# Float32 products of a first projection split into three float32r products each, with low parts and a power table on GpSimd

## The reference

```python
h = rms_norm(x, even_mix_norm[j])
proj = jnp.einsum('bld,de->ble', h, even_in_proj[j])        # 1024 -> 512 + 4 x 512
u = proj[..., :S5_WIDTH]                                    # state-space mixer
hq, hf, hi, hg = jnp.split(proj[..., S5_WIDTH:], 4, axis=-1) # query, forget, value, gate
a_out = s5_mixer(u, s5_lambda_re[j], ...)     # diagonal complex scan, powers of A in tables
b_out = hgrn2_mixer(hq, hf, hi, hg, lower_bounds[layer], hgrn_o_norm[j])
mix = jnp.einsum('bld,de->ble', jnp.concatenate([a_out, b_out], axis=-1), even_out_proj[j])
...
x = x + mix   # then a mixture of 16 experts; then layer 1: windowed attention and 16 experts
```

## Time and profile before

| what | value |
|---|---|
| time, median of 3 runs (lowest to highest) | 841.51 us (840.99 to 843.66) |
| profiled execution, first to last instruction | 839.3 us |
| instructions | 11097 |
| busy: PE, DVE, ACT, POOL | 788.2, 599.7, 467.4, 165.9 us |
| mean granted TensorE clock | 0.982 |
| chain that ended last: PE, DMA, DVE, ACT, POOL | 51%, 22%, 14%, 8%, 1% |

### The profile page before, as it was taken

One profiled execution on the slowest core, in us unless ns is written; L12 is line 12 of the kernel. 1 busy time (PEld: TensorE's weight loads), 2 busy tenths in 40 slices (PEclk: granted clock), 3 DMA queues, 4 the chain that ended last, 5 costly groups with the idle time before them and its releaser, 6 DMA issues.

```text
span 839.3 us, 11097 instructions
## 1 busy us (share of the span) xinstructions
PE 788.2 (94%) x4236; PEld 553.6 (66%) x4236; DVE 599.7 (71%) x817; ACT 467.4 (56%) x637; POOL 165.9 (20%) x169
## 2 busy tenths in 40 slices
PE   5999999999999899988998999999999899999992
PEld 3455555555688878867876555556579778777771
DVE  4699974766553879877996466757635798797890
ACT  5033202814333488786885118676735488697781
POOL 4400001400001222322211001033102223234121
PEclk9999999999999899999999999999998899999997
DMA  9422020203453499989986300142064599999952
GB/s 370 155 91 73 30 101 1 101 1 138 192 211 125 164 421 357 333 316 313 329 306 229 125 0 1 37 165 100 1 276 166 207 397 351 316 320 333 325 162 33
DMA packets 31451, 160.94 MB, mean 192 GB/s; under 512 B 7601, under 2 KB 7729, under 8 KB 16032
## 3 DMA queue, kind: packets, MB, share of 16 engines
q1 hardware_dynamic: 18432, 130.03, 40.6%
q0 software_dynamic: 11232, 24.60, 10.4%
q10 hardware_dynamic: 1728, 5.52, 1.7%
HBM read 152.32 MB, written 24.12 MB: 210 GB/s over the span
## 4 chain that ended last, share of the span: by engine, by line
PE 51%; DMA 22%; DVE 14%; ACT 8%; POOL 1%; issue 1%; DVEq 0%; ACTq 0%; SPq 0%; POOLq 0%
DMA ring<-stream 21%; PE PS L1795 11%; DVE w_lo L992 9%; PE PS L1982 8%; PE PS L2231 7%; PE PS L1761 3%; ACT w_hi L686 3%; PE PS L2012 2%; PE PS L2137 2%; PE PS L2112 2%; PE PS L2266 2%; PE PS L1927 2%; PE PS L2289 1%; PE PS L2045 1%; PE PS L1745 1%
## 5 line engine op out<-in xcount | busy, mean ns | idle before, releaser
L992 DVE TENSOR_TENSOR w_lo<-ring,w_hi 128x2048 fp32r<-128x2048 f32 x92 | 210.0, 2290 | 40.8 <-ACT w_hi L686 37.4
L686 ACT ACTIVATE w_hi<-ring 128x2048 fp32r<-128x2048 f32 x86 | 164.7, 1917 | 47.2 <-DMA ring<-stream 43.4
L2112 PE MATMUL PS<-w_hi,left_hi 128*128 128x512 f32 x512 | 174.4, 402 | 6.1 <-DVE w_lo L992 3.7
L2112 PEld LDWEIGHTS PS<-w_hi,left_hi 128*128 128x128 f32 x512 | 96.2, 188 | 29.2 <-DVE w_lo L992 6.0
L2112 PE MATMUL PS<-w_lo,left_hi 128*128 128x512 f32 x256 | 100.2, 391 | 0.0
L2137 PE MATMUL PS<-w_hi,left_lo 128*128 128x512 f32 x256 | 85.3, 394 | 9.6 <-DVE left_lo L992 8.4
L2231 PE MATMUL PS<-ring,hT 128*128 128x512 f32 (+1 forms) x192 | 74.6, 534 | 0.0
L536 POOL DMA_INDIRECT arena<-rows x32 | 49.6, 1549 | 122.8 <-PE PS L2089 108.6
L2137 PEld LDWEIGHTS PS<-w_hi,left_lo 128*128 128x128 f32 x256 | 48.1, 188 | 22.4 <-DVE left_lo L992 11.0
L1795 PE MATMUL PS<-ring,hT 128*128 128x512 f32 x128 | 57.6, 599 | 0.4 <-ACT arena L732 0.4
L1795 PE MATMUL PS<-hT,ring 128*128 128x512 f32 x128 | 56.3, 595 | 0.0
(11 more groups left out here) (274 smaller groups left out, 1373.2 us busy)
## 6 DMA issues: line engine op xcount, KB each, us to landing
ring<-stream SPq DMA_DIRECT2D x110, 1024.0 KB, 16.3
arena<-stream SPq DMA_DIRECT2D x6, 1024.0 KB, 8.1
rows<-arena POOLq DMA_DIRECT2D x8, 512.0 KB, 3.0
x<-stream SPq DMA_DIRECT2D x4, 1024.0 KB, 6.6
x<-x_in SPq DMA_DIRECT2D x4, 512.0 KB, 5.5
x<-x_in ACTq DMA_DIRECT2D x4, 512.0 KB, 4.5
sums<-x POOLq DMA_DIRECT2D x4, 512.0 KB, 3.8
x<-sums SPq DMA_DIRECT2D x4, 512.0 KB, 5.2
```

What stands on the lines that cost most here:

```text
L686: act.activation(w_hi[pair], held_slot(layer, m), ACT.Copy).then_inc(w_hi_done, 1)
L992: return V.tensor_tensor(out, a, b, op)
L2112: ins = mm(PS[:, gate_bank(e), :], a, b, start=k == 0 and t == 0, stop=k == KD - 1 and t == 2)
```

## The change

The u blocks 1 to 3 and the blocks of `proj(0)` to `proj(7)`, 11 blocks, become split blocks of 24 float32r matmuls (`block_products`). u block 0, value and gate blocks stay in float32.

The parts that this needs:

- ScalarE makes the high parts of 11 blocks (`block_hi(j)`, 128x1024 each), some into spare memory, blocks 5 to 11 over the first two ring slots.
- VectorE makes the high part of `hT` (`hT_hi`, two casts of 128x2048), the low parts of weight blocks 1 to 3, and `left_lo` = hT - hT_hi (two operations of 128x2048), all ahead of its tiny preparation operations.
- GpSimd makes the low parts of blocks 4 to 11 (`block_lo(j)`), the read-out power table (`read_powers`, six operations of 128x2048, in place of VectorE), and writes `hT` anew as hT_hi + left_lo once block 11 is finished, for `proj(8)` and later.
- On TensorE `turn_inputs` now stands behind two blocks, `inputs(1)` stands directly behind `make_taps`. Ring slots 0 to 5 are released from the last split block on.
- `IN_COEF` is now the third count of its semaphore, and `READ_COEF` a count of GpSimd's. Some semaphores of the routing are merged (`weigh_done`), with the same waits.

```diff
+            def block_lo(j):
+                pool.wait_ge(in_hi_done, j)
+                nc.gpsimd.tensor_tensor(in_lo(j), in_raw(j), in_hi(j), ALU.subtract).then_inc(in_lo_done, 1)
+            def read_powers():
...
+                TT_(out_re, c_re, a_re, ALU.mult)
+                TT_(t, c_nim, a_im, ALU.mult)
+                pool.drain()
+                TT_(out_re, out_re, t, ALU.add)
+                TT_(out_im, c_nim, a_re, ALU.mult)
+                block_lo(6)
+                block_lo(7)
+                pool.drain()
+                TT_(t, c_re, a_im, ALU.mult)
+                pool.drain()
+                TT_(out_im, out_im, t, ALU.subtract).then_inc(turns_done, 1)
+            nc.gpsimd.tensor_scalar(read_nim[:, 0, :], read_nim[:, 0, :], -1.0, None, ALU.mult)
+            block_lo(4)
+            block_lo(5)
+            pool.wait_ge(coefs_done, POWERS)
+            pool.drain()
+            read_powers()
+            for j in range(8, 12):
+                block_lo(j)
+            for half in range(2):
+                ks = slice(4 * half, 4 * half + 4)
+                pool.wait_ge(proj_psum, 8)
+                nc.gpsimd.tensor_tensor(hT[:, ks, :], hT_hi[:, ks, :], left_lo[:, ks, :], ALU.add).then_inc(in_lo_done, 1)
...
+            for j in range(5, 9):
+                block_hi(j)
...
             projected(0)
+            projected(1)
+            block_hi(9)
             act.wait_ge(coefs_done, PHASE)
...
-            for i in range(1, 10):
+            block_hi(10)
+            for i in range(2, 10):
                 projected(i)
+                if i == 3:
+                    block_hi(11)
...
+            dve.drain()
+            for half in range(2):
+                ks = slice(4 * half, 4 * half + 4)
+                V.tensor_copy(hT_hi[:, ks, :], hT[:, ks, :]).then_inc(first_lo_done, 1)
+            for j in range(1, 4):
+                dve.wait_ge(in_hi_done, j)
+                tt_(in_lo(j), in_raw(j), in_hi(j), ALU.subtract)
+            dve.drain()
+            dve.wait_ge(u_psum, 1)
+            for half in range(2):
+                ks = slice(4 * half, 4 * half + 4)
+                tt_(left_lo[:, ks, :], hT[:, ks, :], hT_hi[:, ks, :], ALU.subtract).then_inc(first_lo_done, 1)
...
-            grown((read_re[:, 0, :], read_nim[:, 0, :]), read_re[:, 1:, :], read_nim[:, 1:, :], read_tmp, STEP, ALU.add, ALU.subtract).then_inc(coefs_done, 1)
...
             products_in(1)
+            scan_and_products(0)
             expand_taps()
-            scan_and_products(0)
...
+                    w, h = (in_hi(j), in_hi(j), in_lo(j))[t], (hT_hi, left_lo, hT_hi)[t]
+                    for k in range(KD):
+                        ins = mm(out, w[:, k, :], h[:, k, :], start=t == 0 and k == 0, stop=t == 2 and k == KD - 1)
...
-            proj(0)
+            split_proj(0)
+            split_proj(1)
             turn_inputs()
-            proj(1)
+            split_proj(2)
             pe.wait_ge(u_done, 4)
             pe.wait_ge(bT_done, 2 * STEP)
             inputs(0)
-            proj(2)
-            proj(3)
+            split_proj(3)
+            split_proj(4)
+            split_proj(5)
             make_taps()
-            proj(4)
             inputs(1)
-            proj(5)
             readout(0)
```

More of the change, by code:

```diff
@@ L714, in _, with block_hi @@
             act.dma_start(read_nim[:, 0, :], cread_d[:, 512:1024]).then_inc(const_rest, 16)
+            def block_hi(j):
+                if j in (1, 4, 8):
+                    for i in (j // 4 * 2, j // 4 * 2 + 1):
+                        full, turn = filled(i)
+                        act.wait_ge(full, 16 * turn)
+                if j == 5:
+                    act.wait_ge(u_psum, 4)
+                if j >= 9:
+                    act.wait_ge(proj_psum, j - 7)
+                act.activation(in_hi(j), in_raw(j), ACT.Copy).then_inc(in_hi_done, 1)
+            for j in range(1, 4):
+                block_hi(j)
             act.wait_ge(turns_done, TURN)
@@ L1752, in _, with block_products @@
                 turn_tile(0, tt)
+            def block_products(j, out, terms=(0, 1, 2)):
+                for t in terms:
+                    if t == 0:
+                        pe.wait_ge(in_hi_done, j)
+                    if t == 2 and j >= 4:
+                        pe.wait_ge(in_lo_done, j - 3)
+                    w, h = (in_hi(j), in_hi(j), in_lo(j))[t], (hT_hi, left_lo, hT_hi)[t]
+                    for k in range(KD):
+                        if t < 2 and j == 1 and k % 4 == 0:
+                            pe.wait_ge(first_lo_done, 2 * t + k // 4 + 1)
+                        ins = mm(out, w[:, k, :], h[:, k, :], start=t == 0 and k == 0, stop=t == 2 and k == KD - 1)
+                        if t == 0 and k == 0:
+                            give(ins)
+                return ins
             full(0)
             full(1)
[L1755 to L1766, removed]
+            for k in range(KD):
+                if k % 4 == 0:
+                    pe.wait_ge(hT_done, 2 * TT - 1 + k // 4)
+                ins = mm(PS[:, 2, :], in_raw(0)[:, k, :], hT[:, k, :], start=k == 0, stop=k == KD - 1)
+            ins.then_inc(u_psum, 1)
+            for cb in range(1, 4):
+                block_products(cb, PS[:, 2 + cb, :], (0,))
+            for cb in range(1, 4):
+                block_products(cb, PS[:, 2 + cb, :], (1, 2)).then_inc(u_psum, 1)
             def turn_inputs():
@@ L1787, in proj @@
                     full(s)
-                    full(s + 1)
                 if i >= 2 and 0 in ks:
@@ L1791, in proj @@
                 for k in ks:
[L1792 to L1793 removed]
+                    if i % 4 == 0 and k == 4:
+                        full(s + 1)
+                    if i == 8 and k % 4 == 0:
+                        pe.wait_ge(in_lo_done, 8 + k // 4 + 1)
                     m = slice((i % 4) * 128, (i % 4) * 128 + 128)
[L1795 removed]
+                    ins = mm(PS[:, 7 if i >= 12 else 6 + i % 2, :], hT[:, k, m], k512(s + k // 4)[:, k % 4, :],
+                             start=k == 0, stop=k == KD - 1)
                     if i % 4 == 3 and k == 3:
@@ L1837, in readout @@
                 for k in range(STEP):
-                    mm(out[:, k * NSTEP:SEQ], taps[:, b, k, :], uT[:, b, 0:SEQ - k * NSTEP], start=k == 0, stop=False)
+                    ins = mm(out[:, k * NSTEP:SEQ], taps[:, b, k, :], uT[:, b, 0:SEQ - k * NSTEP], start=k == 0, stop=False)
+                    if k == 0:
+                        give(ins)
                 pe.wait_ge(state_done, b + 1)
```

87 lines of the change are left out of this document (59 added, 28 removed).

## The result

The changed kernel takes **874.29 us** (median of 4 runs, 871.29 to 875.51) against 842.31 us of the kernel before on the same chips (4 runs, 840.99 to 843.66): a ratio of 1.0368, 95% interval 1.0345 to 1.0392. It is slower by 32.0 us. The profiled execution has a span of 873.7 us (839.3 before).

A forecast was written before the change was run, and what follows sets the result against it. The prediction took the stage as bound by TensorE (94% busy). Lateness 35.9 - 3.0 + 2.1 = 35.0; span 839.3 + 35.0 + 1.0 (clock) = 875.3, with 2.2 to the median 877.5 us, range 863 to 885.

The forecast's parts named there:

- VectorE and GpSimd as one resource: Both take turns after each operation where VectorE reads two SBUF operands or makes a plain float32 pass; PSUM products run free.
- The late magnitude: GpSimd's tiny magnitude operations are held back by VectorE's seven new ones; VectorE goes on at 36.7 us, not 27.64.
- the rival of free tiny operations: GpSimd's tiny magnitude operations pass VectorE's freely: 8 us less, 869.5 us; chance 0.15.
- The length of a turn: GpSimd's turns between VectorE's table operations: multiply 3.5 us, add 4.5, low part 2.25; input table done at 81.2.
- turns are shorter: Rival: GpSimd's turns on VectorE's path, about 43 us, are 6 less: 871.5 us, or 865 with free tiny operations; chance 0.15.
- To the first read-out: From the fifth forget-and-query block at 115.4, VectorE ready at 134.0, TensorE at 132.0: `readout(0)` 35.9 us late.
- the two split blocks: Behind the first read-out, two split blocks in place of two of 13.93 us together gain 3.0 us.
- `proj(8)`: Waits for both halves of the rewritten hT, adds of 4.5 us each; with the scans' delay it loses 2.1 us.
- The clock: TensorE drops to the lower clock behind the two new standstills; about 1 us of the second loss stays.
- Downstream: Later stages give none of the lateness back, as transfers that bind afterwards start late by the same: no gain counted.

The follow-up runs named there:

- experiment 1: Changed kernel with each added GpSimd operation replaced by two zero fills of the same target, so GpSimd writes but reads nothing (results wrong): 834.46 us, ratio 0.9921.
- experiment 4: Kernel before, all in float32, with only the read-out power table (negation and six operations) moved to GpSimd: 860.17 us, ratio 1.0217.
- experiment 6: Changed kernel with the low parts, read-out table and rewritten hT made by VectorE instead of GpSimd, nothing left out: 855.7 us, ratio 1.0171.
- Experiment 5: Changed kernel with GpSimd's exponential of the magnitude replaced by a fill with 0.97, so the magnitude is early and wrong: 866.81 us, ratio 1.0299.
- experiment 8: Changed kernel with 250 unread transposes keeping TensorE busy, 170 before `turn_inputs` and 80 before the fifth forget-and-query block: 872.55 us, ratio 1.0373.
- experiment 3: Changed kernel without GpSimd's added work: third product of blocks 4 to 11 rereads the high part, table and hT zero-filled: 838.54 us, ratio 0.9958.
- experiment 7: Changed kernel with GpSimd's added work and the magnitude's exponential on VectorE, high parts of hT on ScalarE, nothing left out: 848.11 us, ratio 1.0077.

## Why the prediction was right, point by point

**Forecast and time.** 877.5 us was forecast and 874.29 measured, 32.0 above the kernel before on the same chips instead of 36.0. In the profiled execution the span was 873.7 against 875.3.

**VectorE and GpSimd as one resource.** Shown by experiments 1, 4 and 6 together: about the same busy time of GpSimd without reads costs nothing against before, one table with reads costs 19 us without any split, and the same work on VectorE alone is 18 to 19 us faster than the change. The products from PSUM ran free, as assumed (2.48 us beside GpSimd). For operations with two operands the rule holds only against GpSimd operations that read, which the prediction did not say. The Trainium skill says it, in "SBUF — State Buffer", section "Who interferes with whom": a VectorE instruction with two SBUF inputs contends with a GpSimd instruction that reads SBUF, not with one that only writes it. Experiment 1 agrees (3.43 and 1.76 us beside the fills). The plain pass with one operand took turns too, as the prediction had it: 3.38 and 3.26 us beside GpSimd's low parts (77.42 and 97.51) instead of 1.22, and it was held up by fills as well.

**The late magnitude.** Forecast at 36.7, was at 35.1 (VectorE goes on at 35.16). Tiny operations waited as forecast, one at each change: 2.03 and 2.10 beside the halves of hT's low part. The 1.5 us too much lie in the count: by 31 us, 18 of the 29 were through and not 15. Experiment 5 gives its price, 7 us, where the rival of free tiny operations had 8.

**The length of a turn** is the term that was mis-sized. From the rows above, length less own length: a multiply 6.89 - 3.43 = 3.46 and 5.04 - 1.76 = 3.28, an add with the multiply behind it 11.15 - 3.58 = 7.57, so some 4.1 for the add, a low part 3.74 - 1.76 = 1.98. The sum had 3.5, 4.5 and 2.25. The spans recorded for GpSimd (5.15 to 5.82) hold VectorE's turn as well and are no measure of this. The distance between GpSimd's starts, less VectorE's usual 1.76, agrees with the turns: 55.84 - 50.68 - 1.76 = 3.40 for a multiply, 66.92 - 61.13 - 1.76 = 4.03 for the add. They are longer than the 3.1 that the prediction scaled up from 128x512, and mostly shorter than what its sum used. Up to the fifth block the forecast was 5.0 too late (115.4 against 110.43). Of this, 1.5 is the magnitude. The turns are nearly all the rest: 1.2 between VectorE's going on and the table (15.4 us, forecast 16.6), 1.0 in the input table (ready at 77.49, forecast 81.2), and 1.2 in the phase table (sine and cosine ready at 108.94, forecast 113.8). The rival "turns are shorter" took off 6 and was thus half true, and the measured time lies about halfway between its 871.5 and the 877.5; together with the other rival's 8 it would be 863.5 and not the 865 given.

**To the first read-out.** Forecast 134.0, or 135.0 with the 1.0 of the clock, which the sum adds at its end. It was 129.90, so 5.1 too much, and all but 0.1 of that was there at the fifth block. But it was not VectorE that came last. The forecast had VectorE at 134.0 and TensorE at 132.0. In the trace nothing waits before the read-out: TensorE needed 19.5 us from the fifth block and not 16.6, mostly because of the clock, and VectorE was done at 128.74, as its last operation for the taps started at 126.26 and took 2.48. So the 31.99 us of lateness stand against a forecast of 36.9.

**Behind it.** Forecast -3.0 for the two split blocks and +2.1 for `proj(8)`. By TensorE's timelines the second read-out starts at 145.15 (115.86 before) and the third at 158.32 (126.95 before). The lateness goes from 32.0 to 29.3 and back to 31.4, so the two terms measure -2.7 and +2.1. The form was right as well (GpSimd's adds of 4.6 and two short waits of 0.89 and 0.92).

**The clock.** Forecast 1 us on the path; experiment 8 shows 1.0 there, of 2.6 that TensorE lost behind the second wait. The prediction did not see the wait of 4.10 us for the low part as a place where the clock falls; it cost nothing.

**Downstream.** Forecast nothing. `turn_head`, the matmuls that turn the first head's output within the output projection, in the chain of the kernel before and in that of the changed one:

```profile
226.75 0.66 PE PS L1969 x4
...
258.10 0.66 PE PS L2090 x4
```

The lateness is still 31.35 us there, and 34.4 at the end. From this point to the end the two profiled executions need 612.6 and 615.6 us. But this rest does not follow the lateness: it is 609.9 us in experiment 1 and 615.9 in experiment 3, which are both early, and 612.1 to 615.0 in the five other traces of kernels that leave nothing out. The profiled execution of the changed kernel is also the second slowest of its four. So the 3 us are within what this rest varies by, and no run shows that they are the change's; the medians differ by 32.0. That the stall isn't given back is settled either way.

**Is there a version that beats both?** No run that does all the work did; the best were 855.7 and 848.11. With GpSimd's work left out, the kernels took 834 and 838, so in this form no more than some 7 us seem to be had. VectorE has no slack before the first read-out: in experiment 7 it makes TensorE wait 4.36 and 4.20 us there although only the raw phase collides any more. Behind the second of these waits the clock was 0.50, and the read-out took 4.63 us instead of 2.42. Low parts that are made later, in VectorE's idle time from 116 us on, would, as I read the program, need SBUF for both halves of hT while hT itself is still read; that wasn't tried.

## What to carry to other kernels

Before work is moved from VectorE to GpSimd to lighten it, look at what VectorE does at that time: where both read operands from SBUF, VectorE waited out each of GpSimd's turns here (2.0 us for a 128x1024 low part that VectorE makes in 1.2), and a chain of tiny operations suffered as much as one of large ones. GpSimd cost VectorE nothing where it only wrote beside two-operand operations (3.43 and 1.76 us), or while VectorE's products read PSUM (2.48 us). And when a bound engine is made cheaper, first ask for the slack of the next one: here 0.8 us at the input table and 3.7 at the read-out (VectorE's work for it ended at 94.32, and it started at 98.07), against 15.5 to be gained.

## What the runs showed that I had not expected

- Fills by GpSimd leave VectorE's two-operand operations at their length (1.76 us for 128x1536) but lengthen its plain pass over 128x2048 from 1.22 to 1.73, and are held up by it in turn (2.72 instead of 1.85).
- Where TensorE's clock falls decides what it costs. Experiment 1 lost some 1.7 us behind a wait of 2.72, with another wait to come, and that cost nothing. Experiment 3, with GpSimd at rest, lost 2.6 us behind a wait of 6.72 on the path, and its first read-out came 1.9 us later.
- Twelve tiny VectorE operations took 1.7 us where GpSimd read nothing, and 8.12 and 6.05 beside its low parts.
